# The feed-forward block in two stages: an up projection with seven block products for eight, its result through DRAM, and a down projection that adds all of ff in PSUM

## The reference, cut to what matters

```python
x = layer_norm(DEEPNORM_ALPHA * x + heads @ w_out, ln_mix_g, ln_mix_b)   # phase d
h = jnp.square(jax.nn.relu(x @ w_ff1))                                   # up: 1024 -> 4096
x = layer_norm(DEEPNORM_ALPHA * x + h @ w_ff2, ln_ffn_g, ln_ffn_b)       # down: 4096 -> 1024
```

## Time and profile before

| | us |
|---|---|
| median of 3 runs (2803.2 to 2806.25) | 2804.89 |
| the profiled execution, its own time | 2812.7 |
| its span in the profile | 2811.0 |
| PE busy | 2623.1 (93%) |
| DVE busy | 1539.8 (55%) |
| ACT busy | 865.8 (31%) |
| POOL busy | 685.8 (24%) |
| phase e, from its first load at 1033.2 to the end | 1777.8 |

### The profile page before, as it was taken

How to read it: one execution, slowest core, us unless ns; L and a number is a source line. 1 busy time by engine, 2 the same in 40 slices (tenths; PEclk the granted TensorE clock), 3 DMA queues, 4 the chain that set the end, 5 groups by cost and what they waited for, 6 DMA issues and landing times.

```text
span 2811.0 us, 36254 instructions
## 1 busy us (share of the span) xinstructions
PE 2623.1 (93%) x12480; PEld 2193.9 (78%) x12480; DVE 1539.8 (55%) x1962; ACT 865.8 (31%) x1457; POOL 685.8 (24%) x460
## 2 busy tenths in 40 slices
PE   3999968599799969999999999999999999999998
PEld 2888757588678858888788888888888888888887
DVE  6322064788655536545665456654566555664546
ACT  2111122577621123222232232322224232232321
POOL 5000020122212232222332224322243222432222
PEclk9999959799899989999999999999999999999999
DMA  5321141522245554323352323532235323253231
GB/s 205 118 104 75 75 151 76 125 68 67 83 164 174 179 186 166 99 96 97 98 180 96 99 91 104 180 99 95 97 98 180 105 90 103 92 187 98 93 101 60
DMA packets 123183, 326.82 MB, mean 116 GB/s; under 512 B 11169, under 2 KB 42913, under 8 KB 121313
## 3 DMA queue, kind: packets, MB, share of 16 engines
q1 hardware_dynamic: 110608, 279.29, 29.5%
q0 software_dynamic: 12496, 46.41, 5.6%
HBM read 260.12 MB, written 65.54 MB: 116 GB/s over the span
## 4 chain that ended last, share of the span: by engine, by line
PE 60%; DVE 1%; POOL 1%; issue 1%; DVEq 0%; ACT 0%; DMA 0%; POOLq 0%; ACTq 0%
PE e_up L42 10%; PE e_up L43 10%; PE e_up L44 10%; PE e_down L42 10%; PE e_down L43 10%; PE e_down L44 10%; DVE e_hid L1376 0%; DVE e_w_lo L1382 0%; POOL e_xt_lo L1298 0%; POOL e_w_lo L1303 0%; POOL e_rstd L1315 0%; DVEq L1399 0%; DMA e_w_raw<-w_ff 0%; DVE e_stats L1401 0%; DVE e_acc L1389 0%
## 5 line engine op out<-in xcount | busy, mean ns | idle before, releaser
L1376 DVE TENSOR_TENSOR e_hid<-e_relu 128x512 f32<-128x512 f32 x160 | 378.9, 2368 | 710.0 <-ACT e_relu L1350 709.9
L1303 POOL TENSOR_TENSOR e_w_lo<-e_w_raw,e_w_hi 128x1024 fp32r<-128x1024 f32 x162 | 395.0, 2438 | 1207.6 <-ACT e_w_hi L1342 1207.6
L1342 ACT CAST e_w_hi<-e_w_raw 128x1024 fp32r<-128x1024 f32 x162 | 170.4, 1052 | 1152.5 <-PE e_up L44 1100.5
L42 PE MATMUL e_up<-e_xt_hi,e_w_lo 128*128 128x512 f32 x1280 | 501.6, 392 | 19.5 <-POOL e_xt_lo L1298 16.1
L42 PE MATMUL e_down<-e_w_hi,e_h_lo 128*128 128x512 f32 x1280 | 498.3, 389 | 3.1 <-DVE e_w_lo L1382 3.1
L43 PE MATMUL e_up<-e_xt_lo,e_w_hi 128*128 128x512 f32 x1280 | 500.4, 391 | 0.0
L44 PE MATMUL e_up<-e_xt_hi,e_w_hi 128*128 128x512 f32 x1280 | 500.1, 391 | 0.0
L44 PE MATMUL e_down<-e_w_hi,e_h_hi 128*128 128x512 f32 x1280 | 498.0, 389 | 0.0
L43 PE MATMUL e_down<-e_w_lo,e_h_hi 128*128 128x512 f32 x1280 | 498.0, 389 | 0.0
L42 PEld LDWEIGHTS e_up<-e_xt_hi,e_w_lo 128*128 128x128 f32 x1280 | 241.8, 189 | 73.7 <-issue 19.8
L42 PEld LDWEIGHTS e_down<-e_w_hi,e_h_lo 128*128 128x128 f32 x1280 | 240.2, 188 | 54.4 <-issue 4.7
(11 more groups left out here) (149 smaller groups left out, 3536.4 us busy)
## 6 DMA issues: line engine op xcount, KB each, us to landing
e_w_raw<-w_ff SPq DMA_DIRECT2D x322, 512.0 KB, 3.4
s_proj<-a_stage SPq DMA_DIRECT2D x50, 256.0 KB, 2.0
a_x_in<-x POOLq DMA_DIRECT2D x20, 512.0 KB, 5.0
s_x_norm<-a_x_nrm SPq DMA_DIRECT2D x20, 512.0 KB, 3.7
c_q_raw<-s_proj POOLq DMA_DIRECT2D x40, 256.0 KB, 4.2
d_h_raw<-s_heads POOLq DMA_DIRECT2D x20, 512.0 KB, 5.0
d_xn<-s_x_norm POOLq DMA_DIRECT2D x20, 512.0 KB, 5.3
s_x<-d_x SPq DMA_DIRECT2D x20, 512.0 KB, 3.9
```

What stands on the lines that cost most here:

```text
L42: tensor.matmul(out, w_lo, m_hi, start=first, stop=False)
L1303: pool.tensor_tensor(w1_lo[:, slot, :], w1_raw[:, slot, :], w1_hi[:, slot, :].bitcast(F32), ALU.subtract).then_inc(w1_split, 1)
L1342: act.copy(w1_hi[:, u % 2, :], w1_raw[:, u % 2, :]).then_inc(w1_hi_done, 1)
L1376: dve.tensor_tensor(hid[:, u % 2, :], relu[:, u % 4, :], relu[:, u % 4, :], ALU.mult)
```

## The change

`mix_out` also produces, for each pair of token tiles, the seven operands that Strassen's scheme (in Winograd's form) needs of the tokens, and stores them in one array `xb` (1792 KB for a pair). ACT copies the four quarters out of PSUM (`take_quarters`), DVE works out the other operands (`mix_quarters`). The two tiles of a pair come from the two halves of an up group. `mlp` is replaced by `mlp_up` and `mlp_down`, with a barrier of all engines between them. `mlp_up` takes three groups of tokens: two of 2 x 512 and one of 2 x 256 tokens. A pair of ff tiles (16 pairs in a group) takes seven products of 4 x 3 matmuls, with 512 columns (256 in the third group). The squared result goes to DRAM (`h`). `mlp_down` reads it back; its 32 units of a group of 512 tokens are added in the eight PSUM banks, and DVE adds the residual only at the end of a group.

```diff
+UP_GROUPS = ((0, 512), (1024, 512), (2048, 256))
+UP_ORDER = (("P1", "A11", "B11"), ("P6", "S2", "T2"), ("P2", "A12", "B21"), ("P5", "S1", "T1"), ("P7", "S3", "T3"),
+            ("P4", "A22", "T4"), ("P3", "S4", "B22"))
...
+            def mix_quarters(q):
+                m = mixed[:, q % 2, :, :]
+                dve.wait_ge(quarters_done, 2 * q + 2)
+                dve.tensor_tensor(m[:, X_SLOT["T1"], :], b12[:], m[:, X_SLOT["B11"], :], ALU.subtract)
+                dve.tensor_tensor(m[:, X_SLOT["T3"], :], m[:, X_SLOT["B22"], :], b12[:], ALU.subtract)
+                dve.drain()
+                dve.tensor_tensor(m[:, X_SLOT["T2"], :], m[:, X_SLOT["B22"], :], m[:, X_SLOT["T1"], :], ALU.subtract)
+                dve.drain()
+                dve.tensor_tensor(m[:, X_SLOT["T4"], :], m[:, X_SLOT["B21"], :], m[:, X_SLOT["T2"], :], ALU.subtract
+                                  ).then_inc(mixed_done, 1)
...
+            for n in range(NT):
+                norm(n)
+                if n + 2 < NT:
+                    rest_of_heads(n + 2)
+                if n % 2 == 0 and n >= 4:
+                    mix_quarters(n // 2 - 2)
+            mix_quarters(NT // 2 - 2)
+            mix_quarters(NT // 2 - 1)
...
+                    sp.dma_start(xb_d[q], mixed[:, q % 2, :, :]).then_inc(mixed_st[q % 2], 16)
...
+def mlp_up(nc, xb_d, w1_d, h_d):
+        x_raw = al.sb("x_raw", [P, 2, 2, 4 * P])
...
+        @block.gpsimd
+        def _(pool):
+            for g in range(len(UP_GROUPS)):
+                for j in range(NPROD):
+                    for i in x_parts(g):
+                        n = x_part(g, j, i)
+                        if n >= 2:
+                            pool.wait_ge(x_split, n - 1)
+                        q = first_pair(g) + 2 * i
+                        pool.dma_start(x_raw[:, n % 2, :, :], xb_d[q:q + 2, :, j, :].rearrange("q p c -> p q c")
+                                       ).then_inc(x_ld[n % 2], 16)
...
+            def w_sums(n, s, first=False):
...
+                dve.tensor_tensor(w_sum[:, 0, :], raw[:, 3, :], raw[:, 2, :], ALU.add)
+                dve.tensor_tensor(w_sum[:, 2, :], raw[:, 0, :], raw[:, 3, :], ALU.subtract)
+                dve.drain()
+                dve.tensor_tensor(w_sum[:, 1, :], w_sum[:, 0, :], raw[:, 0, :], ALU.subtract)
+                dve.drain()
+                dve.tensor_tensor(w_sum[:, 3, :], raw[:, 1, :], w_sum[:, 1, :], ALU.subtract).then_inc(w_summed, 1)
...
+            def body(g, p, s, end):
+                n, w = g * NP + p, UP_GROUPS[g][1]
+                more = not (end and g == LAST)
+                turn = end and more
+                wb_low(n, s)
+                if turn:
+                    x_low(g + 1, 0)
+                dve.wait_ge(prod_done, n * NPROD + 2)
+                dve.wait_ge(p1_done, n + 1)
+                dve.wait_ge(c_read[12], n + 1)
+                dve.tensor_tensor(u2[:, 0:w], bank[:, s, BANK["P6"], 0:w], p1[:, 0:w], ALU.add).then_inc(u2_done, 1)
+                if turn:
+                    x_low(g + 1, 1)
+                if more:
+                    w_sums(n + 1, 1 - s)
+                    wa_low(n + 1, 1 - s)
+                if turn:
+                    x_low(g + 1, 2)
+                    x_low(g + 1, 3)
+                dve.wait_ge(prod_done, n * NPROD + 5)
+                dve.wait_ge(c_read[21], n + 1)
+                dve.tensor_tensor(u3[:, 0:w], bank[:, s, BANK["P7"], 0:w], p1[:, 0:w], ALU.add).then_inc(u3_done, 1)
+                dve.drain()
+                dve.wait_ge(c_read[22], n + 1)
+                dve.tensor_tensor(c22[:, 0:w], bank[:, s, BANK["P5"], 0:w], u3[:, 0:w], ALU.add
+                                  ).then_inc(c_done[22], 1)
...
+            x_low(0, 0)
+            w_sums(0, 0, True)
+            wa_low(0, 0)
+            for j in range(1, NPROD):
+                x_low(0, j)
+            pairs(dve, body)
...
+            def body(g, p, s, end):
+                n, w = g * NP + p, UP_GROUPS[g][1]
+                more = not (end and g == LAST)
+                turn = end and more
+                act.wait_ge(prod_done, n * NPROD + 1)
+                act.wait_ge(u3_done, n + 2)
+                act.copy(p1[:, 0:w], bank[:, s, BANK["P1"], 0:w]).then_inc(p1_done, 1)
+                if turn:
+                    x_high(g + 1, 0)
+                    x_high(g + 1, 1)
+                act.wait_ge(prod_done, n * NPROD + 3)
+                relu(n, 11, bank[:, s, BANK["P2"], 0:w], w)
+                if more:
+                    wa_high(n + 1, 1 - s)
+                square(n, 11, w)
+                if turn:
+                    x_high(g + 1, 2)
+                    x_high(g + 1, 3)
+                finish(n, 22, c22[:, 0:w], w)
+                if turn:
+                    x_high(g + 1, 4)
+                finish(n, 21, u3[:, 0:w], w)
+                if turn:
+                    x_high(g + 1, 5)
+                    x_high(g + 1, 6)
+                if more:
+                    act.wait_ge(prod_done, n * NPROD + NPROD)
+                    wb_high(n + 1, 1 - s)
+                finish(n, 12, u2[:, 0:w], w)
...
+                    elif prod == "P2":
+                        pe.wait_ge(p1_done, n + 1)
+                    elif prod == "P5":
+                        pe.wait_ge(c_done[12], n + 1)
+                    elif prod == "P7":
+                        pe.wait_ge(u2_done, n + 1)
+                        pe.wait_ge(wb_split, n + 1)
+                    elif prod == "P4":
+                        pe.wait_ge(c_done[21], n + 1)
+                    else:
+                        pe.wait_ge(c_done[22], n + 1)
+                    pe.wait_ge(x_split, x_part(g, j, x_parts(g)[-1]) + 1)
...
+def mlp_down(nc, x1_d, h_d, w2_d, ln_g, ln_b, out_d):
+    NU = FF // P
+    HEAD = 2 * TPG
+    R = 4
...
+            units(dve, 0, low, 0)
+            dve.wait_ge(const_in, 32)
+            add_residual(0)
+            with dve.Fori(1, NG) as g:
+                for u in range(HEAD):
+                    low(g, u, u % R)
+                    if u % 2 == 0:
+                        moments(g - 1, u // 2)
+                    else:
+                        normalise(g - 1, u // 2)
+                units(dve, g, low, HEAD)
+                add_residual(g)
...
+            def unit(g, u, s):
+                pe.wait_ge(split, g * NU + u + (R + 1))
+                for o in range(2 * TPG):
+                    tok, cols = slice((o // 2) * P, (o // 2 + 1) * P), slice((o % 2) * 512, (o % 2 + 1) * 512)
+                    if isinstance(u, int) and u == 0:
+                        pe.wait_ge(summed, g * 2 * TPG + (o + 1))
+                    mm = split_mm(pe, bank[:, o, :], h_hi[:, s, tok], h_lo[:, s, tok], w_hi[:, s, cols],
+                                  w_lo[:, s, cols], isinstance(u, int) and u == 0,
+                                  isinstance(u, int) and u == NU - 1)
+                mm.then_inc(unit_done, 1)
```

More of the change, by code:

```diff
@@ L1105, in norm @@
                 dve.drain()
-                if first and s == 0:
+                if n == 0:
                     dve.wait_ge(const_in, 48)
@@ L1140, in product @@
                             pe.wait_ge(h_split, n + 1)
[L1141 removed]
+                            if n >= 2:
                                 pe.wait_ge(y_done, n - 1)
[L1143 removed]
+                        if n == 0 and h == 0:
                             pe.wait_ge(w_split, k + 1)
@@ L1229, in mlp, with units @@
         y_done, y_st = al.sem("y_done"), al.sems("y_st", TPG)
-        DOWN0 = NO + 1
+        passed = al.sem("passed")
         block = ctx.enter_context(nc.Block())
-        def chunks(eng, g, body):
-            with eng.Fori(1, NC // 2) as i:
-                for s in range(2):
-                    body(g, i * 2 + s, s)
+        def units(eng, g, body, start):
+            with eng.Fori(start // R, NU // R) as i:
+                for s in range(R):
+                    body(g, i * R + s, s)
@@ new lines, in _ @@
+            sp.dma_start(gain[:], ln_g.partition_broadcast(P)).then_inc(const_in, 16)
+            sp.dma_start(shift[:], ln_b.partition_broadcast(P)).then_inc(const_in, 16)
+            for t in range(TPG):
+                load_x1(0, t)
+            units(sp, 0, load, HEAD)
+            with sp.Fori(1, NG) as g:
+                for u in range(HEAD):
+                    load(g, u, u % R)
+                for s in range(R):
+                    load(g, HEAD + s, s)
+                for t in range(TPG):
+                    store_y(g - 1, t)
+                units(sp, g, load, HEAD + R)
+                for t in range(TPG):
+                    load_x1(g, t)
@@ L1398, in norm, with low, add_residual @@
-            def norm(g, t):
+            def low(g, u, s):
+                dve.wait_ge(hi_done, g * NU + u + 1)
+                dve.tensor_tensor(h_lo[:, s, :], h_raw[:, s, :], h_hi[:, s, :].bitcast(F32), ALU.subtract)
```

(21 more changed lines are left out.)

609 lines of the change are left out of this document (314 added, 295 removed).

## The result

The changed kernel took 2936.3 us (median of 4 runs, 2930.9 to 2938.2), the kernel before 2805.5 (4 runs, 2803.2 to 2806.3): 1.0465 times as long, interval 1.0446 to 1.0483. 2946 had been forecast. The profiled execution has a span of 2932.8 us, where before had 2811.0.

The account below looks back on a forecast made before the run. PE, busy 93% of the span, was taken as the bound. Up 957.4 and down 945.2 made 1902.6 for 1777.8 (+124.8); with phase d's +16.3, +141 on 2804.9 gave 2946 us, range 2875 to 3020.

Parts of the forecast that it names:

- Phase d: DVE's four subtractions, 3.0 us per two tiles with 0.5 spare: growth 8 us, end 8.3 later, +16.3 in all.
- The seven products for eight: Wide groups of `mlp_up`: 1344 matmuls each for 1536, 87.0 us saved; 19.03 us a pair, P3's chain hidden.
- rival (d): Weight-sum adds in `mlp_up` take 2.52 us instead of 0.68: +320 us, 3266; chance 0.02.
- The third group: 256-column group of `mlp_up`: PE waits for `c22` before P3; chain 13.8 us, 15.0 taken a pair, 240 in all.
- The allowance for the clock: Third group of `mlp_up`: a pair lies between 13.8 and 18.1 us (half clock), taken as 15.0.
- The loads: Token loads in `mlp_up`, 5.0 us each, 7.5 a round: first pair ends at 73, turns lose 34 and 13.
- The end of `mlp_up`: Behind the last product: `finish`, the store of `h` and the barrier, 7.5 us.
- The down phase: `mlp_down`: start 9.0, matmuls 870.1, four group ends of 9.6 each (38.4), tail 27.7; 945.2 us in all.
- Rival (b): Milder: loads land in 3.4 us (-24), third group at 13.8 or less (-19 to -79): 2843 to 2903; chance 0.14.
- (c): Worse: clock drops in each pair of the third group (+50), rounds take 9 us (+22): 3018; chance 0.11.
- Rival (e): Faster: ACT's and DVE's hand-offs run ahead, nothing PE waits for in `mlp_up` is late: 163 less, 2783; chance 0.05.

Follow-up runs that it names:

- The first experiment: Changed kernel with `mix_quarters` moved ahead of `rest_of_heads(n + 2)` in DVE's program of phase d: 2906.4 us, ratio 1.036 to the kernel before.
- the last version: Version of 2801.4 us (helpful edits combined, groups 512/384/384, operands split in place, ACT's weight copy earlier) with ACT's and DVE's work reordered in four places: 2782.1 us, ratio 0.9906.
- four slots: Changed kernel with `mlp_up`'s token operands loaded in parts of 256 KB through four slots instead of 512 KB through two: 2918.0 us, ratio 1.0398.
- one unit ahead: Changed kernel with DVE splitting the next group's first unit in `mlp_down` before the eight residual adds instead of behind them: 2923.0 us, ratio 1.0421.
- two gave 31: Changed kernel with the next group's first two units in `mlp_down` split on DVE ahead of the eight residual adds: 2905.0 us, ratio 1.035.

## Why the prediction was right, and where it was not

The time was inside the range and 10 us below the forecast. That is better than its terms were. Phase d with its end was 17 us too short in the sum and `mlp_up` 38 too long, which partly cancel. As spans the forecast was 19 us high (2952 for 2932.8). That the medians differ by only 10 is luck: the profiled execution of the kernel before, from which the terms were read, ran 7.8 us above its median, the changed kernel's 1.4 below its own.

- **Phase d, the step that failed.** "Two tiles share the delay: each pair of tiles alternates short and long steps and grows by about 1 us, 8 in all." It grew by 283.3 - 251.8 = 31.5 us, and nothing was shared. Seven of the `mix_quarters` stand ahead of a `norm` whose `rstd` lets a later tile load, and behind each of them PE waits once, 2.1 to 4.8 us for `h_lo`, 22.9 us in all. Behind five of the seven waits came half clock, for which the step had no term: 18.8 us of the phase's matmuls start some 0.43 us apart, where before had 3.0, which makes some 8 us (an estimate from these spacings). The first experiment shows that it was the order, as the same subtractions ahead of `rest_of_heads` gave 30 back, waits and clock together. The end of the phase was 6.1 us later (8.3). What is ahead of phase d was 3.9 shorter in this pair of profiles, where the change does nothing; that was not looked into.
- **The seven products for eight.** Right: 19.04 us a wide pair, with no wait at P3, so the operand in four blocks costs nothing. The adds of the weight sums took 0.69 us each (0.68), so rival (d) fell. This agrees with the Trainium skill ("SBUF — State Buffer", Practical consequences), by which a VectorE instruction with two SBUF inputs contends with a GpSimd one that reads SBUF: beside these adds GpSimd only issued loads.
- **The third group.** The place of the wait was right (`c22`, P3). The group took some 27 us less than 240, and the part that was too large is the chain: 12.6 us a pair where the clock stayed whole, for 13.8. That is what its rows alone had added up to: in the sum the 1.2 us for eight hand-offs, an estimate, were not needed. The allowance for the clock, 1.2 us, was right in size: 1.0 to 1.2 us in 12 pairs of 15.
- **The loads.** The places were right, and so, nearly, were the sizes: the first pair ended at 71.0 us (73), the first turn lost 32.7 (34), the second 8 (13). The load was 4.0 us, not 5.0. The Trainium skill ("DMA: Bandwidth & Descriptors", Anatomy of one DMA) would have had 3.2 for these 512 KB: the measured figure lies between its price and the row's, and with 3.2 alone the sum would have come out 27 us lower.
- **The end of `mlp_up`.** From the end of its last matmul to the first load of `mlp_down` were 4.4 us (7.5).
- **The down phase.** 946.1 for 945.2. The first matmul came 7.8 us after the first load (7.2), a turn held PE 6.9 us (7.8) with 3.0 to 6.1 us of half clock behind it (3.6), and from the last matmul (begun at 2905.29) to the end were 27 us (27.7).

Rival (b) was half right: the third group fell in it, and the loads lay halfway. Of (c) the clock did fall, in 12 of 15 pairs of the third group, but for some 3.5 us and not for the whole pair: about 13 us in all, which are inside the forecast's own allowance, and not 50 more. Its rounds of 9 us did not come. Rival (e), that the hand-offs are hidden and the change gains, failed for this kernel; that the last version came to 2782.1, with the orders changed, groups of 384 and another loading, is a coincidence with its 2783: 49.4 us of waits are still in it.

Where the gain went: PE alone was to give 100 us, and the kernel lost 131, so some 230 us went into waits and half clock. Experiments put 128 of them in four places: 30 in the order of phase d, 42 at the turns of `mlp_up`, 25 in the order of the third group, 31 at the turns of `mlp_down`. The rest, some 100 us, was not taken out by itself. By the traces, which count and do not prove, it lies in four more places. The start of `mlp_up`: the first pair ends 71.0 us after the first load, 52 later than its 19 us of matmuls, where phase e had some 10 for its start (and the slow clock); four slots made its P2 10 us earlier. The third group, which even in its own order stays 1.9 us a pair above its matmuls, 30 in all. The new border between `mlp_up` and `mlp_down`, 4.4 + 7.8 us. And the tail behind the last matmul, 27 us where the kernel before had 10.3.

## What to carry to other kernels

Fewer matmuls on an engine that is 93% busy pay only if what feeds them is hidden, so look at each start and each change of group for what stands ahead of the awaited instruction in its engine's own order: here order alone was worth 30, 25, 31 and 19 us. When a wait is moved away, ask at once what is late next: one unit ahead gave 13.5 us, two gave 31. An insertion of 3 us in a cycle with 0.5 us to spare cost 31.5 us in seven rounds, 4.5 each: more than itself, as half clock came behind most of the waits. So price a wait of PE with the clock behind it.

## What was not expected of the hardware

The clock does not fall with each hole, and the length of the hole alone does not decide it. Windows of 2 us at the first turn of `mlp_down`: in the changed kernel PE stands for 6.9 us and the granted clock is at half, the lower level of 1.2 GHz, when it starts again; with one unit ahead (the second fence) it stands for 3.25 us, from about 2179.6 to 2182.9, and the clock stays whole.

```profile
2176.00:2178.00 2.00, 0.00 (x0) 0.00 (x0) 2.00 (x4) 0.00 (x0) 0.00 (x0) 0.50 0.00 0
2178.00:2180.00 2.00, 1.29 (x3) 1.11 (x4) 1.85 (x3) 0.00 (x0) 0.00 (x0) 0.50 0.11 12
```

```profile
2180.00:2182.00 2.00, 0.00 (x0) 0.00 (x0) 2.00 (x3) 1.32 (x2) 1.46 (x1) 1.00 0.00 0
2182.00:2184.00 2.00, 1.11 (x5) 0.92 (x6) 1.79 (x2) 0.00 (x0) 0.00 (x0) 1.00 0.00 0
```

A hole of nearly the same length, 3.14 us, near the start of `mlp_up` did bring it down, and only after PE had started again (the last version's timeline): the first matmul's record is short, the fourth's is of the half clock, for 3.4 us.

```profile
1067.72 0.47 PE L57 MATMUL u_bank<-u_x_hi,u_wa_lo 128*128 128x512 f32 x1 [3.14 <-DVE u_x_lo L1316]
...
1068.52 0.63 PE L57 MATMUL u_bank<-u_x_hi,u_wa_lo 128*128 128x512 f32 x1
...
1071.90 0.39 PE L59 MATMUL u_bank<-u_x_hi,u_wa_hi 128*128 128x512 f32 x1
```

Ahead of that hole PE had run for only 8 us after a stand of 26.7; ahead of the other for a whole group, but for a hole of 0.9 us some 9 us before. That difference alone does not explain it. In phase d of the changed kernel PE had run for some 25 us ahead of each of these two holes, and the shorter one is followed by half clock, the longer one is not:

```profile
922.08 0.79 PE L57 MATMUL d_mix<-d_w_hi,d_h_lo 128*128 128x512 f32 x1 [2.41 <-DVE d_h_lo L1107]
...
950.67 0.50 PE L57 MATMUL d_mix<-d_w_hi,d_h_lo 128*128 128x512 f32 x1 [3.17 <-DVE d_h_lo L1107]
```

```profile
922.00:924.00 2.00, 1.92 (x5) 1.54 (x6) 1.91 (x5) 0.00 (x0) 0.00 (x0) 0.52 0.04 8
...
952.00:954.00 2.00, 2.00 (x11) 1.64 (x10) 1.82 (x4) 0.00 (x0) 0.36 (x2) 1.00 0.00 0
```

The next hole there, 3.77 us at 978.51, left the clock whole too, while in the third group 1.82 us brought it down again and again. What decides it these runs do not show.
